# The small gate columns of a hybrid decoder layer: 24 split matmuls of 96 columns replaced by 8 plain fp32 matmuls of 32 columns in four column groups, and one matmul that adds the groups up

## The reference, cut to what matters

```python
xn = rmsnorm(x, mix_norm_g)
p = xn @ w_in                                   # 1024 -> 10256 columns
(aq, ak, av, ao, ai, af, bb, bc, bx, cz, cxbc, cdt, sq, sk, sv, gates) = split(p)
ya = mlstm(aq, ak, av, ao, ai + a_igate_b, af + a_fgate_b, a_norm_g)   # ai, af: 4 columns each
yc = mamba2_mixer(cz, cxbc, cdt, ...)                                  # cdt: 8 columns
yd = stick_breaking_attention(sq, sk, sv)                              # "D" below, 4 heads
```

## Time and profile before

| what | value |
|---|---|
| median of 3 runs | 1036.73 us (1036.67 to 1036.95) |
| the profiled execution's own time | 1038.42 us |
| its span | 1036.7 us |
| PE busy | 1019.0 us, 98% of the span |
| DVE busy | 593.2 us, 57% |
| ACT busy | 424.3 us, 41% |
| mean granted TensorE clock | 0.992 |

### The profile page before, as it was taken

The page is one execution under the profiler, slowest core; times in us unless marked ns, Lnnn a source line. Parts: engine busy times, 40 slices in busy tenths (PEclk is TensorE's granted clock), DMA queues, the critical chain, the costliest instruction groups (busy, mean ns, idle before and its releaser), DMA issues.

```text
span 1036.7 us, 12635 instructions
## 1 busy us (share of the span) xinstructions
PE 1019.0 (98%) x4724; PEld 837.8 (81%) x4724; DVE 593.2 (57%) x764; ACT 424.3 (41%) x515; POOL 67.6 (7%) x74
## 2 busy tenths in 40 slices
PE   8999999999999999999999999989999999999996
PEld 7897888887777887777888888868888888888886
DVE  6835754656676566556364456687656666543323
ACT  5514445644435322444432333544444344332331
POOL 5610000000000000000000000320000000000002
PEclk9999999999999999999999999989999999999998
DMA  6332222223222333343252222513233222253312
GB/s 238 114 113 70 82 84 82 77 93 105 89 85 82 120 122 124 132 132 103 81 183 87 97 88 97 181 61 119 85 100 101 100 86 88 68 176 94 102 56 81
DMA packets 32024, 108.24 MB, mean 104 GB/s; under 512 B 3684, under 2 KB 5860, under 8 KB 31600
## 3 DMA queue, kind: packets, MB, share of 16 engines
q1 hardware_dynamic: 29520, 93.86, 27.1%
q0 software_dynamic: 2320, 13.69, 4.0%
q10 hardware_dynamic: 144, 0.14, 0.1%
HBM read 103.42 MB, written 4.25 MB: 104 GB/s over the span
## 4 chain that ended last, share of the span: by engine, by line
PE 93%; DVE 4%; ACT 2%; issue 1%; DMA 1%; DVEq 0%; SPq 0%; ACTq 0%
PE gb L413 81%; PE gb L446 4%; DVE w_lo L985 1%; PE xb L596 1%; PE gb L524 1%; PE xb L556 1%; PE xb L549 1%; PE xb L536 1%; PE xb L413 1%; ACT w_hi L701 1%; PE xb L513 1%; DMA raw<-w_stream 1%; DVE y_lo L993 1%; PE gb L464 1%; PE xb L584 0%
## 5 line engine op out<-in xcount | busy, mean ns | idle before, releaser
L985 DVE TENSOR_TENSOR w_lo<-raw,w_hi 128x1024 fp32r<-128x1024 f32 (+2 forms) x181 | 218.1, 1206 | 342.8 <-ACT w_hi L701 342.4
L701 ACT ACTIVATE w_hi<-raw 128x1024 fp32r<-128x1024 f32 (+2 forms) x181 | 183.8, 1017 | 413.5 <-PE gb L413 380.8
L413 PE MATMUL gb<-xn_hi,w_hi 128*128 128x512 f32 x720 | 285.0, 396 | 0.0
L413 PE MATMUL gb<-xn_hi,w_lo 128*128 128x512 f32 x720 | 281.1, 390 | 0.0
L413 PE MATMUL gb<-xn_lo,w_hi 128*128 128x512 f32 x720 | 281.0, 390 | 0.0
L413 PE MATMUL gb<-y_hi,w_hi 128*128 128x512 f32 x400 | 159.1, 398 | 6.0 <-DVE y_lo L993 4.2
L413 PEld LDWEIGHTS gb<-xn_hi,w_hi 128*128 128x128 f32 x720 | 135.8, 189 | 29.7 <-issue 1.0
L413 PEld LDWEIGHTS gb<-xn_lo,w_hi 128*128 128x128 f32 x720 | 135.8, 189 | 29.0 <-issue 1.4
L413 PEld LDWEIGHTS gb<-xn_hi,w_lo 128*128 128x128 f32 x720 | 135.6, 188 | 28.6
L413 PE MATMUL gb<-y_lo,w_hi 128*128 128x512 f32 x400 | 156.6, 391 | 0.0
L413 PE MATMUL gb<-y_hi,w_lo 128*128 128x512 f32 x400 | 156.4, 391 | 0.0
(11 more groups left out here) (231 smaller groups left out, 1018.4 us busy)
## 6 DMA issues: line engine op xcount, KB each, us to landing
raw<-w_stream SPq DMA_DIRECT2D x149, 512.0 KB, 3.3
raw<-w_down SPq DMA_DIRECT2D x16, 384.0 KB, 3.0
abc<-scr_a POOLq DMA_DIRECT2D x8, 640.0 KB, 4.1
raw<-w_down SPq DMA_DIRECT2D x16, 320.0 KB, 2.8
x_in<-xT SPq DMA_DIRECT2D x8, 256.0 KB, 6.5
x<-xT POOLq DMA_DIRECT2D x1, 2048.0 KB, 8.5
scr_x<-x POOLq DMA_DIRECT2D x1, 2048.0 KB, 7.4
x<-scr_x POOLq DMA_DIRECT2D x1, 2048.0 KB, 8.4
```

The source lines that it names most:

```text
L413: ins = pe.matmul(out, w[:, r, lo:hi], rhs(k)[x], start=(first and n == 0 and q == 0), stop=(last_ and n == len(ks) - 1 and q == 2))
L701: act.activation(w_hi[:, r, 0:n], raw[:, r, 0:n], ACT.Copy).then_inc(S["hi_ready"], 1)
L985: dve.tensor_tensor(w_lo[:, r, 0:n], raw[:, r, 0:n], w_hi[:, r, 0:n].bitcast(F32), ALU.subtract)\
```

## The change

The three products of each slab of unit 12 become one plain fp32 matmul of 32 weight columns, of which 16 are used. Slab k goes to column group k mod 4 of the array, so its result lands on partitions 32(k mod 4) and up. After the eight matmuls four partial sums stand side by side on 128 partitions. DVE copies them out (`g_in`), and a matmul with `sel`, a matrix of zeros and ones, adds the four and puts the rows where the old matmul had them. The weights are not split: DVE multiplies them by the norm's gain (`w_small`), and the moving operand is `x_in`, the normalised input without gain. ACT still makes the unit's `w_hi`. With the extra matmul behind unit 13, the work on the gates moves by one unit on DVE and ACT.

```diff
+    sel = m.put("sel", [P, 96])
+    w_small = m.put("w_small", [P, KD, P // NCOL])
@@ POOL
-        pool.wait_ge(S["xn_ready"], KD)
+        pool.wait_ge(S["unit_done"], U_SMALL + 1)
         pool.memset(g_one[:], 1.0).then_inc(S["masks"], 1)
@@ PE, unit(u)
             elif u == U_SMALL:
-                for k in range(KD):
-                    for q, (w, x) in enumerate(((w_hi, 0), (w_hi, 1), (w_lo, 0))):
-                        ins = pe.matmul(gb(o)[0:96, :], w[:, u % RING, P * k:P * k + 96], xn(k)[x],
-                                        start=(k == 0 and q == 0), stop=(k == KD - 1 and q == 2))
+                for n in range(KD // NCOL):
+                    for c in range(NCOL):
+                        k = NCOL * n + c
+                        w = P // NCOL
+                        ins = pe.matmul(gb(o)[w * c:w * c + w, :], w_small[:, k, :],
+                                        x_in[:, k, :], start=(n == 0), stop=(n == KD // NCOL - 1),
+                                        skip_group_check=True)
@@ PE, loop over u
+            if u == U_SMALL + 1:
+                pe.wait_ge(S["g_sel"], 1)
+                pe.wait_ge(S["psum_read_dve"], order[first_tile[U_SMALL]][1])
+                pe.matmul(GB[3][0:96, :], sel[:], g_in[:], start=True, stop=True).then_inc(S["g_sum"], 1)
@@ ACT, loop over u
-            if s == 14:
+            if s == 15:
                 table(EXP_LN)
-                act.wait_ge(S["psum_read_dve"], order[first_tile[U_SMALL]][1])
+                act.wait_ge(S["g_split"], 1)
-            if s == 20:
+            if s == 21:
@@ DVE
+        def small_gain(u, r):
+            dve.wait_ge(S["hi_ready"], u + 1)
+            dve.tensor_tensor(w_small[:], raw[:, r, :].rearrange("p (k c) -> p k c", k=KD)[:, :, 0:P // NCOL],
+                              vec[:, V_MIX:V_MIX + KD].unsqueeze(2).to_broadcast([P, KD, P // NCOL]), ALU.mult)\
+                .then_inc(S["lo_ready"], 1)
@@ DVE, evac(u)
             elif u == U_SMALL:
-                dve.wait_ge(S["masks"], 5)
-                dve.wait_ge(S["rsm_loaded"], 16)
-                link(dve.tensor_scalar(g_i[:], ps[0:4, :], rsm[0:4, 0:1], None, ALU.add))
-                link(dve.tensor_scalar(g_x[0:4, :], ps[32:36, :], rsm[0:4, 1:2], -1.0, ALU.add, ALU.mult))
-                dve.tensor_scalar(g_x[32:40, :], ps[64:72, :], rsm[32:40, 1:2], None, ALU.add)\
-                    .then_inc(S["psum_read_dve"], 1)
+                read(dve.tensor_copy(g_in[:], ps[:, :]))
@@ DVE, loop over u
-            if s == 15:
+            if s == 9:
+                link(dve.memset(sel[:], 0.0))
+                ...        # three reductions of the identity into sel
+            if s == 14:
+                dve.wait_ge(S["g_sum"], 1)
+                ...        # the three tensor_scalars of before, out of GB[3]
+            if s == 16:
                 dve.wait_ge(S["g_log"], 2)
-            if s == 17:
+            if s == 18:
                 link(dve.tensor_tensor(g_row[0:4, :], g_i[:], g_b[0:4, :], ALU.add))
-            if s == 19:
+            if s == 20:
                 for j in range(NB):
```

More of the change, by code:

```diff
@@ L45 @@
 LINE = 512
+NCOL = 4
 A_HEADS, C_HEADS, D_HEADS = 4, 8, 4
@@ L215, in build @@
     sp_hi = g.put("sp_hi", [P, PACK], F32R)
+    g_in = g.put("g_in", [P, T])
     assert g.at <= C0 + 12 * 4 * T
@@ L252, in build @@
         d_scores d_masked d_soft_in d_soft d_sp_hi d_sp_lo d_suffix d_expo d_weights d_out d_hi d_lo
-        g_log g_rows g_en g_trans g_cols rows_out a_out
+        g_sel g_sum g_split g_log g_rows g_en g_trans g_cols rows_out a_out
         a_nm a_en a_arg a_dec a_scores a_w a_wsum a_numden a_h a_sq a_sum a_rstd a_y a_hi a_lo
@@ L519, in _ @@
                     pe.wait_ge(S["d_lo"], h)
+                else:
+                    pe.wait_ge(S["g_split"], 1)
                 if h == 2:
@@ L1104, in _ @@
         for u in range(U_OUT):
-            if u < U_OUT - 1:
+            if u + RING == U_SMALL:
+                small_gain(u + RING, u % RING)
+            elif u < U_OUT - 1:
                 lo(u + RING, u % RING)
@@ L1144, in _ @@
                 split_lo(y_lo[0][:, h, :], GB[3][:, :], y_hi[0][:, h, :]).then_inc(S["d_lo"], 1)
-            if s == 15:
+            if s == 9:
+                dve.wait_ge(S["masks"], 3)
+                link(dve.memset(sel[:], 0.0))
+                rows = ident[:].rearrange("p (c r) -> p r c", c=NCOL)
+                for r0, n, c0 in ((0, 4, 0), (4, 4, 32), (8, 8, 64)):
+                    ins = dve.tensor_reduce(sel[:, c0:c0 + n], rows[:, r0:r0 + n, :], mybir.AxisListType.X, ALU.add)
+                    if r0 < 8:
+                        link(ins)
+                ins.then_inc(S["g_sel"], 1)
+            if s == 14:
+                dve.wait_ge(S["masks"], 5)
+                dve.wait_ge(S["rsm_loaded"], 16)
+                dve.wait_ge(S["g_sum"], 1)
+                ps = GB[3]
+                link(dve.tensor_scalar(g_i[:], ps[0:4, :], rsm[0:4, 0:1], None, ALU.add))
+                link(dve.tensor_scalar(g_x[0:4, :], ps[32:36, :], rsm[0:4, 1:2], -1.0, ALU.add, ALU.mult))
+                dve.tensor_scalar(g_x[32:40, :], ps[64:72, :], rsm[32:40, 1:2], None, ALU.add)\
+                    .then_inc(S["g_split"], 1)
+            if s == 16:
                 dve.wait_ge(S["g_log"], 2)
@@ L1425, in lay_out @@
     small = np.zeros((D, P), np.float32)
-    small[:, 0:4], small[:, 32:36], small[:, 64:72] = ai, af, cdt
+    small[:, 0:4], small[:, 4:8], small[:, 8:16] = ai, af, cdt
     stream[U_SMALL] = slabs(small)
```

## The result

| | before | changed |
|---|---|---|
| median of 6 runs | 1037.12 us | 1041.51 us (1040.67 to 1041.90) |
| profiled execution, its span | 1036.7 us | 1040.0 us |
| PE busy | 1019.0 us | 1017.9 us |

The changed kernel takes 1.0039 times as long (95% interval 1.0027 to 1.0050), 2.8 to 5.2 us more. The ratio is worked out from all runs and is not that of the two medians, which differ by 4.4 us (0.42%). The spans of the two profiled executions differ by 3.3 us. PE has less to do than before and ends later.

A forecast was written before the change was run, and what follows sets the result against it. PE, busy 1019.0 of 1036.7 us, was taken to bound the kernel. The median 1036.73 plus 1.92 net PE delay behind unit 19 plus 1.4 for the clock gave 1040.0 us; whole range 1038.3 less 0.3 to 1041.8.

The forecast's parts named there:

- Unit 12 at 1.9 us: Unit 12 on PE, 5.52 us before, takes 1.9 us with all four column groups running together.
- The rule on weight loads: Unit 12: loads overlap matmuls in flight only where row groups differ; by it unit 12 would take 4.1 us.
- The first wait: Behind unit 12, head 0's scores wait for DVE's last dv copy, starting at 82.53; gain 1.76 us, not 3.6.
- The term of 0.05 us: At the first wait, the time a DVE result takes to reach PE, taken from the av copy.
- the rival of the other side: Behind unit 12: dv copies done by 80.7, no wait, gain 3.6 instead of 1.76 us; 1036.8 us; chance 0.03.
- The adding matmul at 0.95: Behind unit 13, the extra matmul costs PE 0.95 us: 0.86 plus about 0.09 for the change of form.
- The stall of head 1: PE's wait at 112.00 for DVE's L1115 disappears, gaining 1.04 us; unit 17 begins at 114.48.
- The second wait: Mid unit 19, PE waits 4.06 us for DVE's av copy behind six gate instructions, resuming at 133.01.
- The clock: In or behind unit 19's wait, it falls to 0.50 for about 3.4 us, costing 1.4 us (0.5 to 1.7).
- `a_run` and the other moved work at nothing: Later block a_run (4.4 us), w_small, sel and POOL memset cost nothing; a_run up to 4 us if cover failed.
- the forecast's own range: Whole kernel, stall and fall of the clock together: 1039.0 to 1040.5 us, chance 0.68.
- two rivals that did not happen: Clock also falls behind unit 12: 1041.6 us, chance 0.06; unit 12's column groups don't run together: 1041.8 us, chance 0.06.

The follow-up runs named there:

- e2_dv_first: e1_six_back with DVE, in step 11, copying dv out of PSUM ahead of unit 15's w_lo instead of behind it; 1033.24 us, ratio 0.9963.
- e1_six_back: The changed kernel with the six gate instructions on DVE put back from step 18 to step 17; 1036.14 us, ratio 0.9985.
- e3_before_six_late: The kernel before with only the later gate places: six instructions in step 18, a_run and copies in 20, ACT's exponential in 21; 1043.18 us, ratio 1.0055.

## Why the prediction was right, point by point

- **Unit 12 at 1.9 us**: 1.86 where nothing hides it (e2_dv_first). The row of two column groups carried over to four. The rule on weight loads that the prediction takes from the Trainium skill ("TensorE: Matmul & The Clock Gate", Part 3, "The mechanism") would have given 4.1 by its working; the 1.86 us of e2_dv_first do not agree with it.
- **The first wait**: scores at 82.53 predicted, 82.55 measured, idle 1.84 us for the copy named. The term of 0.05 us from DVE's result to PE was too small here: the copies end at 82.40, so it took 0.15. Taking the copies forward gave the missing part back (1.9 us in the traces, 0.9985 to 0.9963 in the runs), as the rival of the other side priced it.
- **The adding matmul at 0.95**: two ordinary steps behind 90.05 would be 90.51, the second matmul of unit 14 stands at 91.37, so it cost 0.86. The 0.09 for a change of form was not there.
- **The stall of head 1 gone**: yes. Unit 17 began at 114.50, predicted 114.48. The execution had started 0.07 us earlier ahead of unit 12 (78.58 against 78.65 for the last matmul of unit 11), which covers for small errors of the terms.
- **The second wait**: PE resumed at 132.95, predicted 133.01; e1_six_back and e3_before_six_late show from both sides that the place of the six instructions makes it.
- **The clock**: that it would fall was right, the size was not: the term was 1.4 with bounds 0.5 and 1.7, and it measured 1.49 in one execution and 2.16 in another. I had built it on the short fall near the start, which follows gaps of 1.2 and 0.7 us and is missing in five of the nine traces. The nearer row, the wait of 4.16 us at 687.20 in the same trace, I had not used: the clock was low for 6.8 us, 5.8 of them behind the wait, which at half rate gives an upper bound of 2.9 us (an estimate).
- **e3_before_six_late** came out at 0.55%, 5.7 us, where 3.8 + 1.5 = 5.3 was expected. Its trace shows the short fall (4.64 us for the 24 matmuls) and a span of 1041.6 us, as long as its other executions (1040.8 to 1041.6), so a longer fall at unit 19 is not what the record points to. The profiled execution before, with 1036.7, is long: the spans of the 21 beside this run have the median 1035.5.
- **`a_run` and the other moved work at nothing**: no wait of PE answers to them in the chain.
- **The sum**: the direction and each place were right, the size was short. 3.3 us were predicted and 3.3 lie between the two spans, but 4.0 by the ratio and 4.4 by the medians between the timed runs. 1041.51 us is above the forecast's own range (1039.0 to 1040.5), in the part of the whole range that had been left to two rivals that did not happen (the clock stayed at 1.00 at the first wait, and the groups ran together). One step of the frame was wrong: I set the median 0.03 us above the span, but an unprofiled execution too takes 1.7 us more than its own span, so the profiled execution before was one of the longer ones, while that of the changed kernel (1040.0) is near the middle of its own (median 1039.75). That the spans agree with the sum to 0.1 us is in part luck. What the remaining 0.7 to 1.1 us are made of is open; falls that last 6.8 us in some executions and 3.4 in others, at unit 19 and near 690, are of that size.

## What to carry to other kernels

In an order written by hand, price a moved block by the slack at its new place, not by its length: 4.05 us of small instructions cost nothing one step earlier, with 5.5 us of DVE idle, and 3.8 us of PE here. When a unit on the bounding engine becomes shorter, look at once for what the next instruction waits for, since only the part of the saving ahead of that wait arrives. And add to a wait of about 4 us on PE what the clock takes when work resumes, read from the wait in the old trace that is nearest in length, wherever it stands. Here moving one number, `s == 18` to `17`, turned a loss of 0.39% into a gain of 0.15%, and reading PSUM ahead of the weight split made it 0.37%.

## What the runs showed of the hardware that was not expected

- Column groups take their instructions independently of the program's order among the groups. With the order 0 0 1 1 2 2 3 3 eight plain fp32 matmuls of 32 columns by 512 took 1.88 us, with 0 1 2 3 0 1 2 3 1.86 us.
- After idle stretches of the same length (3.82 us by the profile) the clock was low for about 3.4 us in one execution, beginning when PE had resumed, and for about 6.8 us in another, beginning about 1.9 us before it resumed. The same kernel pays 1.5 or 2.2 us for the same wait. In twelve waits of 3.8 to 4.2 us in nine traces the stay was one of these two lengths each time.
